# Rotary exchanges and five norm sums as pairs of fp32r products, with the key's exchange and the exponential's table moved

## What is computed

```python
def rmsnorm(x, g):
    y = xf * lax.rsqrt(jnp.mean(xf * xf, axis=-1, keepdims=True) + EPS)
    return (y * g).astype(x.dtype)

def rope(x, pos):
    x1, x2 = jnp.split(x, 2, axis=-1)
    return jnp.concatenate([x1 * cos - x2 * sin, x2 * cos + x1 * sin], axis=-1)

def shared_kv(h, norm_g, w_dkv, lat_norm, pos):
    ckr = rmsnorm(h, norm_g) @ w_dkv
    c = rmsnorm(ckr[..., :KV_LORA_RANK], lat_norm)
    kr = rope(ckr[..., KV_LORA_RANK:], pos)
    return c, kr

def mla_query(hn, w_dq, q_norm, w_uq, w_uk, pos):
    cq = rmsnorm(hn @ w_dq, q_norm)
    q = (cq @ w_uq).reshape(B, L, N_HEADS, QK_NOPE_DIM + QK_ROPE_DIM)
    q_nope, q_rope = q[..., :QK_NOPE_DIM], q[..., QK_NOPE_DIM:]
    q_rope = rope(q_rope, pos)
```

## Time and profile before

| | |
|---|---|
| median of 3 runs | 736.26 us (736.14 to 736.47) |
| the profiled execution's own time | 736.79 us |
| its span, first to last instruction | 735.1 us |
| TensorE busy | 725.5 us, 99% |
| VectorE, ScalarE, GpSimd busy | 42%, 56%, 73% |
| mean granted TensorE clock | 0.998 of full speed |

### The profile page before, as it was taken

The page is one execution under the profiler, slowest core; times in us unless marked ns, Lnnn a source line. Parts: engine busy times, 40 slices in busy tenths (PEclk is TensorE's granted clock), DMA queues, the critical chain, the costliest instruction groups (busy, mean ns, idle before and its releaser), DMA issues.

```text
span 735.1 us, 16687 instructions
## 1 busy us (share of the span) xinstructions
PE 725.5 (99%) x6255; PEld 709.1 (96%) x6255; DVE 306.8 (42%) x777; ACT 408.4 (56%) x743; POOL 534.9 (73%) x252
## 2 busy tenths in 40 slices
PE   9999999999999999999999999999999999999995
PEld 8999999999999999999999888799999999999995
DVE  5446986233333222232488766753233333221002
ACT  7877555455444444555677576665554444444542
POOL 4895778869878888889868122149878878888891
PEclk9999999999999999999999999999999999999999
DMA  7864455656777755566576898326546555556641
GB/s 260 260 207 139 134 169 176 201 173 211 241 238 231 235 186 173 199 200 203 174 255 192 263 386 310 134 68 218 174 148 198 183 186 180 191 171 197 203 146 60
DMA packets 44842, 144.68 MB, mean 197 GB/s; under 512 B 5650, under 2 KB 6674, under 8 KB 44530
## 3 DMA queue, kind: packets, MB, share of 16 engines
q1 hardware_dynamic: 44498, 143.50, 59.3%
q0 software_dynamic: 144, 0.40, 0.1%
q10 hardware_dynamic: 144, 0.02, 0.0%
HBM read 142.42 MB, written 1.48 MB: 196 GB/s over the span
## 4 chain that ended last, share of the span: by engine, by line
PE 95%; DVE 2%; ACT 1%; DMA 1%; issue 0%; SPq 0%; DVEq 0%; ACTq 0%
PE ps L1373 29%; PE ps L1374 29%; PE ps L1375 29%; PE ps L1774 1%; PE ps L1750 1%; PE ps L1694 1%; DMA h<-xT 1%; PE ps L1503 1%; PE ps L1621 0%; PE ps L1754 0%; PE ps L1412 0%; PE ps L1680 0%; ACT whi L480 0%; DVE ps L851 0%; PE ps L1682 0%
## 5 line engine op out<-in xcount | busy, mean ns | idle before, releaser
L414 POOL TENSOR_TENSOR wlo<-raw,whi 128x1024 fp32r<-128x1024 f32 x221 | 527.1, 2409 | 182.5 <-ACT whi L480 182.4
L1373 PE MATMUL ps<-xhi,whi 128*128 128x264 f32 x1000 | 286.9, 287 | 0.0
L1374 PE MATMUL ps<-xlo,whi 128*128 128x264 f32 x1000 | 283.3, 283 | 0.0
L1375 PE MATMUL ps<-xhi,wlo 128*128 128x264 f32 x1000 | 283.2, 283 | 0.0
L480 ACT ACTIVATE whi<-raw 128x1024 fp32r<-128x1024 f32 x221 | 232.7, 1054 | 50.5 <-PE ps L1375 48.3
L1374 PEld LDWEIGHTS ps<-xlo,whi 128*128 128x128 f32 x1000 | 188.5, 189 | 0.2
L1373 PEld LDWEIGHTS ps<-xhi,whi 128*128 128x128 f32 x1000 | 188.3, 188 | 0.3
L1375 PEld LDWEIGHTS ps<-xhi,wlo 128*128 128x128 f32 x1000 | 187.6, 188 | 0.0
L1373 PE MATMUL ps<-ahi,whi 128*128 128x264 f32 x352 | 100.0, 284 | 0.0
L1375 PE MATMUL ps<-ahi,wlo 128*128 128x264 f32 x352 | 99.9, 284 | 0.0
L1374 PE MATMUL ps<-alo,whi 128*128 128x264 f32 x352 | 99.9, 284 | 0.0
(11 more groups left out here) (266 smaller groups left out, 1148.8 us busy)
## 6 DMA issues: line engine op xcount, KB each, us to landing
raw<-w_stream SPq DMA_DIRECT2D x221, 512.0 KB, 3.4
pg<-pages SPq DMA_DIRECT2D x64, 288.0 KB, 4.5
pg<-w_ukT SPq DMA_DIRECT2D x1, 2048.0 KB, 9.3
pg<-w_uv SPq DMA_DIRECT2D x1, 2048.0 KB, 10.0
h<-xT SPq DMA_DIRECT2D x4, 264.0 KB, 4.7
raw<-w_stream SPq DMA_DIRECT2D x4, 256.0 KB, 5.5
y_out<-raw SPq DMA_DIRECT2D x4, 198.0 KB, 2.3
wsraw<-wsT SPq DMA_DIRECT2D x1, 512.0 KB, 5.6
```

Source lines behind the costliest of these rows:

```text
L414: pool.tensor_tensor(wlo[:, c % RING, :], raw[:, c % RING, :], whi[:, c % RING, :].bitcast(F32), ALU.subtract).then_inc(lo_ready, 1)
L1373: pe.matmul(out, whi_, mhi, start=start, stop=False)
L1374: pe.matmul(out, whi_, mlo, start=False, stop=False)
L1375: return pe.matmul(out, wlo_, mhi, start=False, stop=stop)
```

## The change

The exchange works on the rotary rows themselves and no longer on their sine product. ScalarE copies them rounded (`rhi`, L746 of the changed kernel), VectorE makes the cosine product (`sq`, L1198) and the rest (`rlo`, L866), and TensorE exchanges both parts with two fp32r products into one bank (L1669, L1670). Then VectorE multiplies by sine in the bank (`query_sine`, L1208) and subtracts (L1214). The key's exchange is made in the same way (`kphi`, `kplo`, L726, L1686), and stands with the sum "lat" behind the second chunk of pair 0 instead of behind the third.

Five sums (all but mix0's) are two fp32r products of ones with the rounded sum and its rest (`total_hi` by ScalarE, L529; `total_lo` by VectorE, L866), so each takes one more instruction on either engine and `acc` stays in bank 5.

The exchange of pair p-1 now stands behind the first chunk of pair p, one by one. The refinement of the norm "lat" moves behind pair 1 on VectorE, the latents to pairs 3 and 4, the exponential's table from behind pair 1 to behind pair 3 on ScalarE, the latents' copies to pairs 5 and 6. GpSimd clears `qsr` instead of VectorE, and the store of the latents is issued three slabs later.

```diff
-        ones = sb("ones", [P, P])
+        ones_r = sb("ones", [P, P], F32R)
+        ones = ones_r[:].bitcast(F32)
...
-        swap = work[:, 6, 0:P]
+        swap_r = sb("swap_r", [P, P], F32R)
+        rhi, rlo = xhi[:, 4:6, :], xlo[:, 4:6, :]
+        kphi, kplo = xhi[:, 6, :], xlo[:, 6, :]
+        total_hi = sb("total_hi", [P, T], F32R)
+        total_lo = sb("total_lo", [P, T], F32R)
+        SPLIT_SUMS = ("ffn0", "mix1", "q", "lat", "ffn1")
...
+            pool.wait_ge(q_done, 1)
+            pool.memset(qsr[:], 0.0).then_inc(qsr_done, 2)
+            splits(PR_S, PR_S + 3)
...
-            splits(PR_S, SLABS)
+            splits(PR_S + 3, SLABS)
...
+            def total_high(name):
+
+                q = NQ[name]
+                act.wait_ge(acc_done, ACC0[q] + NORMS[q][2])
+                act.wait_ge(sum_done, q)
+                act.activation(total_hi[:], acc, ACT.Copy).then_inc(total_hi_done, 1)
+
+            def gained(name, at, last=False):
                 act.activation(xhi[:, at, :], h[:, at, :], ACT.Copy,
                                scale=gn[:, G[name], at, :]).then_inc(xhi_done, 1)
+                if last:
+                    total_high(name)
...
+            total_high("lat")
+            act.wait_ge(krs_done, 1)
+            act.activation(kphi, ps[:, 3, 0:T], ACT.Copy).then_inc(krhi_done, 1)
...
+                wait_query(act, 3 * p)
+                if p > 1:
+                    act.wait_ge(rope_swap, p - 1)
+                act.activation(rhi[:, p % 2, :], ps[:, 0, 0:T], ACT.Copy).then_inc(rope_hi, 1)
                 for e in range(2):
                     x = 3 * p + 1 + e
+                    if e and p == 0:
+                        root("lat")
...
-            root("lat")
             act.wait_ge(krsum_done, 1)
             act.activation(krhi, ps[:, 5, 0:NP_], ACT.Copy).then_inc(krhi_done, 1)
             act.activation(kr[:], ps[:, 5, 0:T], ACT.Copy).then_inc(kr_done, 1)
             done = queries(1, done)
-            table(ACT.Exp)
-            for g in range(1, PAIRS // 2):
-                turned_queries(2 * g - 2)
-                turned_queries(2 * g - 1)
-                done = queries(2 * g, done)
-                if g == 2:
+            turned_queries(0)
+            for p in range(2, PAIRS):
+                done = queries(p, done)
+                turned_queries(p - 1)
+                if p == 3:
+                    table(ACT.Exp)
+                if p == 5:
                     act.wait_ge(c_done, KL)
                     act.activation(cThi[:], ps[:, 6:8, 0:NP_], ACT.Copy).then_inc(cthi_done, 1)
-                done = queries(2 * g + 1, done)
-                if g == 2:
+                if p == 6:
...
+                whole = last and not any(q == NQ[name] for name in SPLIT_SUMS)
+                dve.tensor_tensor(total[:] if whole else acc, acc, sq[:, m % 2, :], ALU.add).then_inc(acc_done, 1)
+
+            def total_low(name):
+
+                q = NQ[name]
+                dve.wait_ge(acc_done, ACC0[q] + NORMS[q][2])
+                dve.wait_ge(total_hi_done, SPLIT_SUMS.index(name) + 1)
+                dve.wait_ge(sum_done, q)
+                lo_of(total_lo[:], acc, total_hi[:]).then_inc(total_lo_done, 1)
...
+                    if z == 0 and m == KD - 1 and name in SPLIT_SUMS:
+                        total_low(name)
...
+            total_low("lat")
             dve.wait_ge(krs_done, 1)
             dve.wait_ge(cqlo_done, KQ)
-            dve.tensor_tensor(Ra, kp, sinb, ALU.mult).then_inc(krsin_done, 1)
-            dve.tensor_tensor(tt[:, 0, :], kp, cosb, ALU.mult).then_inc(psum_read, KQ + 3)
+            dve.wait_ge(krhi_done, 1)
+            dve.tensor_tensor(tt[:, 0, :], kp, cosb, ALU.mult).then_inc(krs_done, 1)
+            lo_of(kplo, kp, kphi).then_inc(psum_read, KQ + 3)
             def keys_turned():
                 dve.wait_ge(krswap_done, 1)
-                dve.wait_ge(psum_read, QA_N)
-                dve.tensor_tensor(ps[:, 5, 0:T], ps[:, 5, 0:T], tt[:, 0, :], ALU.add).then_inc(krsum_done, 1)
+                dve.tensor_tensor(ps[:, 5, 0:T], ps[:, 5, 0:T], sinb, ALU.mult).then_inc(krs_done, 1)
+                dve.wait_ge(krs_done, 3)
+                dve.tensor_tensor(ps[:, 5, 0:T], tt[:, 0, :], ps[:, 5, 0:T], ALU.subtract).then_inc(krsum_done, 1)
             def keys_turned_low():
                 dve.wait_ge(krsum_done, 1)
                 kr_ready(dve)
-                dve.wait_ge(krhi_done, 1)
+                dve.wait_ge(krhi_done, 2)
...
-                dve.tensor_tensor(tt[:, 1 + p % 2, :], ps[:, 0, 0:T], sinb, ALU.mult).then_inc(rope_sin, 1)
+                dve.wait_ge(rope_hi, p + 1)
                 dve.tensor_tensor(sq[:, p % 2, :], ps[:, 0, 0:T], cosb, ALU.mult).then_inc(rope_cos, 1)
+                lo_of(rlo[:, p % 2, :], ps[:, 0, 0:T], rhi[:, p % 2, :]).then_inc(rope_lo, 1)
             def query_low(p, e):
                 dve.wait_ge(qnhi_done, 2 * p + e + 1)
                 lo_of(olo[:, 2 * p + e, :], ps[:, 1 + e, 0:T], ohi[:, 2 * p + e, :]).then_inc(qlow_done, 1)
+            def query_sine(p):
+
+                dve.wait_ge(rope_swap, p + 1)
+                dve.tensor_tensor(turned_bank(p), turned_bank(p), sinb, ALU.mult).then_inc(rope_sin, 1)
+
             def query_turned(p):
                 dve.wait_ge(rope_cos, p + 1)
-                dve.wait_ge(rope_swap, p + 1)
-                dve.tensor_tensor(turned_bank(p), turned_bank(p), sq[:, p % 2, :], ALU.add).then_inc(qr_done, 1)
+                dve.wait_ge(rope_sin, p + 1)
+                dve.tensor_tensor(turned_bank(p), sq[:, p % 2, :], turned_bank(p), ALU.subtract).then_inc(qr_done, 1)
             def query_turned_low(p):
...
             query_rope(0)
             query_low(0, 0)
+            keys_turned()
             query_low(0, 1)
-            keys_turned()
-            inverse_root("lat", Rc)
             keys_turned_low()
-            query_rope(1)
-            query_low(1, 0)
-            query_low(1, 1)
-            for g in range(1, PAIRS // 2):
-                query_turned(2 * g - 2)
-                query_turned(2 * g - 1)
-                query_rope(2 * g)
-                query_turned_low(2 * g - 2)
-                query_low(2 * g, 0)
-                query_turned_low(2 * g - 1)
-                query_low(2 * g, 1)
-                if g == 1:
-                    latents(0)
-                query_rope(2 * g + 1)
-                query_low(2 * g + 1, 0)
-                if g == 1:
-                    latents(1)
-                if g == 2:
-                    dve.memset(qsr[ROPE:P, 0], 0.0).then_inc(qsr_done, 1)
-                    dve.memset(qsr[0:ROPE, 1], 0.0).then_inc(qsr_done, 1)
-                if g == 3:
+            for p in range(1, PAIRS):
+                query_rope(p)
+                query_sine(p - 1)
+                query_low(p, 0)
+                query_turned(p - 1)
+                query_low(p, 1)
+                query_turned_low(p - 1)
+                if p == 1:
+                    inverse_root("lat", Rc)
+                if p in (3, 4):
+                    latents(p - 3)
+                if p == 6:
                     latents_low()
-                query_low(2 * g + 1, 1)
-            for p in (PAIRS - 2, PAIRS - 1):
-                query_turned(p)
-            query_turned_low(PAIRS - 2)
+            query_sine(PAIRS - 1)
+            query_turned(PAIRS - 1)
...
-                pe.matmul(ps[:, 4, 0:T], ones[:], total[:], start=True, stop=True).then_inc(sum_done, 1)
+                if name not in SPLIT_SUMS:
+                    pe.matmul(ps[:, 4, 0:T], ones, total[:], start=True, stop=True).then_inc(sum_done, 1)
+                    return
+                n = SPLIT_SUMS.index(name) + 1
+                pe.wait_ge(total_hi_done, n)
+                pe.matmul(ps[:, 4, 0:T], ones_r[:], total_hi[:], start=True, stop=False)
+                pe.wait_ge(total_lo_done, n)
+                pe.matmul(ps[:, 4, 0:T], ones_r[:], total_lo[:], start=False, stop=True).then_inc(sum_done, 1)
...
+                    pe.wait_ge(rope_lo, p)
...
-                pe.wait_ge(rope_sin, p + 1)
+                pe.wait_ge(rope_hi, p + 1)
+                pe.wait_ge(rope_lo, p + 1)
+                pe.wait_ge(swap_done, 4)
                 if p == 0:
                     pe.wait_ge(psum_read, QA_N)
                 elif p == 1:
...
                     kr_ready(pe)
                 else:
                     pe.wait_ge(qrlo_done, 2 * p - 2)
-                pe.matmul(turned_bank(p), swap, tt[:, 1 + p % 2, :], start=True, stop=True).then_inc(rope_swap, 1)
+                pe.matmul(turned_bank(p), swap_r[:], rhi[:, p % 2, :], start=True, stop=False)
+                pe.matmul(turned_bank(p), swap_r[:], rlo[:, p % 2, :], start=False, stop=True).then_inc(rope_swap, 1)
             def queries(p):
                 for z in range(3):
                     query_chunk(p, z)
+                    if p and z == 0:
```

(56 more changed lines are left out.)

4 lines of the change are left out of this document (2 added, 2 removed).

## The result

The changed kernel takes 738.05 us (median of 13 runs, 737.52 to 738.99) against 736.32 for the kernel before in the same session. The ratio is 1.0024, with a 95% interval of 1.0016 to 1.0031: slower by 0.24%, 1.7 us by the medians. The profiled execution took 737.88 us with a span of 736.1 (before: 736.79 and 735.1).

A forecast was written before the change was run, and what follows sets the result against it. TensorE's given work bounds the kernel. Waits of 0.33 + 1.1 + 1.6 + 0.3 + 0.6 + 0.4 = 4.3 us, less 2.84 saved, add 1.45 to 736.26: 737.7 us, range 735.2 to 739.4.

The forecast's parts named there:

- What is taken off TensorE, 2.84 us: Fourteen f32 products become 28 fp32r products; each pair takes 0.24 us instead of 0.445, saving 2.84 us in all.
- Sums at nothing: At the five sums, the two extra instructions are hidden behind the next stage's first chunk; cost nothing, otherwise 0.8 us each.
- Key's exchange, 0.33 us: Behind pair 0's second chunk, TensorE waits for `kplo`, ready at 372.52 when it comes at 372.35; 0.33 us with release and restart.
- What a stop costs beside its wait, 0.06 and 0.1 us: At each TensorE stop, 0.06 us for the release and 0.1 us for the restart are added.
- Pair 1's loop, 1.1 us: Three dependent refinement instructions make the loop 4.49 us against 3.5; TensorE stops 1.1 us at pair 3's first chunk.
- Pair 3's loop, 1.6 us: Slab and table's load on ScalarE make the loop 5.01 us against 3.5; TensorE stops 1.6 us at pair 5's first chunk.
- Pairs 4 and 5, 0.3 us: One more instruction in each loop (second `latents`, latents' rounded copy) gives 3.6 us; about 0.3 us for both.
- three signs of being wrong: No wait at pair 5; waits at pairs without extra work (plain loop over 3.5 us); or a sum that waits.
- Last exchange, 0.6, and scores, 0.4: Pair 6's `cT` and `latents_low` delay the last exchange 0.6 us; VectorE's remaining work delays the scores 0.4 us.
- the parts are ready in time: Rival: ScalarE and VectorE catch up in the query stage, only the 2.84 us saving stands; 733.4 us, chance 0.15.
- Every stop costs more: Rival: seven stops cost 0.25 us more each, or pairs behind pair 3 wait 0.3 each; 739.4 us, chance 0.30.
- A longer hold by the table's load: Rival: the load waits for earlier ScalarE writes, 1.3 us more in pair 3; 739.0 us, chance 0.10.

The follow-up runs named there:

- reordered kernel: Also called the last kernel: changed kernel with all 28 fp32r products, extra pieces moved out of the pairs' loops and the table's load behind the query stage; 733.99 us, ratio 0.9970.
- the load in pair 1's loop: Changed kernel with the exponential's table loaded ahead of pair 0's turned rows instead of in pair 3's turn; 739.38 us, ratio 1.0041.
- the sums alone: Kernel before, with only the five sums as pairs of fp32r products, all exchanges f32 and in place; 734.95 us, ratio 0.9981.
- the spread refinement: Changed kernel with the three refinement instructions of "lat" placed one each in pairs 1, 2 and 3; 736.92 us, ratio 1.0009.
- the f32 sums: Changed kernel with the five sums made as f32 products again, all exchanges kept as changed; 738.43 us, ratio 1.0029.

## Why the prediction came out

It said 737.7 us, and it was 738.05. The mechanism of the forecast was right. The stops were a tenth too small (4.33 us for 4.74), and the 0.2 us in the attention weren't in it. So the net loss was put at 1.5 us and is 2.1 from sum to sum and 1.7 by the medians; that the two times lie only 0.35 us apart is in part luck. The forecast gave "within 0.2%" a little more than "slower" (0.44 and 0.41), and the time came out just on the slower side. Point by point:

- **What is taken off TensorE, 2.84 us.** Held. The pairs run 0.12 us apart; five sums alone brought 1.15 us from sum to sum (1.5 by the medians) where 1.02 was worked out.
- **Sums at nothing.** Held for their own waits. In ffn0 `total_lo` was there well before TensorE came:

```profile
161.24 0.43 DVE L866 TENSOR_TENSOR total_lo<-ps,total_hi 128x264 fp32r<-128x264 f32 x1
```

  It ends at 161.67, and the sum starts at 162.07: 0.4 us ahead of TensorE, as forecast (both times are 0.5 us earlier than forecast because this trace has a shorter head). Without the split of "q" and "lat", though, the key's exchange doesn't stop and the stage is 0.45 us shorter. I counted their instructions in the key's stop but not what they do to the pairs behind.
- **Key's exchange, 0.33 us.** It was 0.40.
- **What a stop costs beside its wait, 0.06 and 0.1 us.** Right, the second by luck. At the two long stops TensorE starts 0.06 us behind the end of VectorE's rest (381.22 to 381.28, 390.04 to 390.10) and loses 0.10 behind the stop. But the row that I took the 0.1 from can't show it: in the earlier trace rows four f32 products stand between the stop and the fp32r product of 0.36 us, and in the kernel before a fp32r product right behind f32 ones has 0.36 us with no wait in its row (the next starts at 411.50):

```profile
411.29 0.36 PE L1373 MATMUL ps<-cThi,whi 128*128 128x256 f32 x1
```

- **Pair 1's loop, 1.1 us.** 1.12, at the place named, and the three refinement instructions stand in front of it in VectorE's order of time (lines 898, 901 and 904):

```profile
379.03 0.44 DVE L898 SCALAR_TENSOR_TENSOR ps<-ps,work 128x264 f32<-128x264 f32 x1
379.51 0.44 DVE L901 SCALAR_TENSOR_TENSOR ps<-ps,work 128x264 f32<-128x264 f32 x1
379.98 0.43 DVE L904 SCALAR_TENSOR_TENSOR work<-ps,work 128x264 f32<-128x264 f32 x1
380.45 0.43 DVE L1198 TENSOR_TENSOR sq<-ps,work 128x264 f32<-128x264 f32 x1
380.80 0.42 DVE L866 TENSOR_TENSOR xlo<-ps,xhi 128x264 fp32r<-128x264 f32 x1
```

  Spread over three pairs they cost this stop no longer.
- **Pair 3's loop, 1.6 us.** The right cause, but a term that was mis-sized: 1.81. ScalarE's and VectorE's order of time show where the 0.2 lie:

```profile
387.24 1.28 ACT L503 ACT_TABLE_LOAD   x1
...
388.75 0.39 ACT L746 ACTIVATE xhi<-ps 128x264 fp32r<-128x264 f32 x1
```
```profile
389.27 0.43 DVE L1198 TENSOR_TENSOR sq<-ps,work 128x264 f32<-128x264 f32 x1 [1.01 <-ACT xhi L746]
389.62 0.42 DVE L866 TENSOR_TENSOR xlo<-ps,xhi 128x264 fp32r<-128x264 f32 x1
```

  The third chunk's reader `qns` starts at 385.09, so time 0 is 384.89. The load starts at 2.35 (predicted 2.36), and 1.51 us pass from it to the next copy, not the 1.40 of the earlier trace rows. VectorE follows that copy after 0.52 us, not 0.42. The two make 0.2. ScalarE is at that copy 0.23 us behind the load's end. The rule of the Trainium skill weighed in the prediction (the page "ScalarE: Activation LUTs", section "What ACT_TABLE_LOAD costs": 1.38 us of drain besides the load's 1.28) doesn't show in this row either.
- **Pairs 4 and 5, 0.3 us.** 0.52, at the first chunks of pairs 6 and 7. Half of the error is in the sum itself: 3.6 us against 3.5 is a wait of 0.1 for each, with the 0.1 of the restart 0.2, so 0.4 for both by the forecast's own prices, and 0.5 with the release. The step also started from a plain loop of 3.02 us, which has the slab behind the first head. With both long pieces away the pairs 4 to 7 still wait 0.1 to 0.4 us each, pair 4 behind a loop that holds nothing extra ahead of the turned rows but the slab of its second head. That is one of the three signs of being wrong that the prediction named, and it is the step that failed in part; in the changed kernel the long stop at pair 3 hides it at pair 4, which doesn't wait there.
- **Last exchange, 0.6, and scores, 0.4.** 0.50 and 0.39.

Of the rivals, "the parts are ready in time" was wrong for the order as it stands. It is nearly what the reordered kernel does (733.99 against 733.4). "Every stop costs more" was wrong in its mechanism: the release and the restart cost what I took. The stops were 0.4 us longer in all, about a quarter of its 1.75, and that came from the terms above. A longer hold by the table's load was right by 0.1 of its 1.3 us.

One step failed in a smaller way in an expectation: that a stop at pair 5 stays whole when time is lost a pair earlier. The stop is counted from pair 3's third chunk, and what TensorE loses between that chunk and pair 5 is taken off it: 1.8 became 1.3 when 0.5 were lost at pair 4. In the changed kernel pair 4 loses nothing, so the prediction's sum wasn't touched.

## What to carry to other kernels

When a change takes work from the engine that bounds, compute the loop that hands a buffer back to it (here: chunk, copies, rests, back to the bank) against the time that the bounding engine now needs for the same turn. Busy shares don't tell: at 82 and 84% busy (26.1 and 26.8 of 32 us) the two helpers stopped TensorE, and at 93 and 89% (27.0 and 25.8 of 29 us), in another order and with the table's load behind the stage, they didn't. Pieces that only have to be done some time (a table's load, a refinement in three dependent steps, copies for a later stage) belong behind the instruction that hands back the buffer, and one per turn. And test the two halves of such a change apart, since here one half alone gained 1.15 us and the rest without it lost 2.2.

## What the chip showed beside

- A stop of TensorE costs about 0.1 us more than its wait. The first fp32r product behind it is recorded with 0.36 to 0.39 us instead of 0.28, and the next starts 0.20 to 0.22 us later instead of 0.12. It was much the same behind a stop of 0.2 us and one of 1.7, and the granted clock of the stretch was 1.00. A fp32r product of 256 columns behind f32 ones shows the same with no wait in its row (0.36 us, the next start 0.21 later, at 411.29 in the kernel before).
- The load of the exponential's table takes 1.28 us each time. Until the next useful instruction 1.40 us pass where that is a copy of 8 or 128 columns (the kernel before, the load in pair 1's loop, the sums alone, the last kernel), and 1.50 to 1.51 where it is the rounding of 264 columns (the changed kernel, the spread refinement, the f32 sums). What makes the 0.1 us wasn't tested.
- Stops of up to 2.4 us in the query stage didn't lower the granted clock of that stretch.
